# Causal attention: how the 1/sum of the softmax gets into the turned exponentials

## Chip, cores and metric

The kernel runs on one core of a Trainium2 chip. The metric is the device time of one execution in microseconds; the median of several runs is compared. The kernel is one program of many stages, of which the attention stage is one.

## What is computed

A first block (two recurrent mixers and a mixture of experts) is followed by a second one, which projects its input and feeds an attention, a state-space mixer and a gated linear recurrence. The change lies in the attention of the second block, cut here to what matters (1024 positions, 8 heads of 64, all float32):

```python
def fox_attention(q, k, v, log_f, q_g, k_g):
    q = rms_norm(q, q_g)
    k = rms_norm(k, k_g)
    c = jnp.cumsum(log_f.astype(jnp.float32), axis=1)
    ...
    def one_block(args):           # 128 queries of every head
        q_i, c_i, blk = args
        logits = jnp.einsum('bhqd,bhkd->bhqk', q_i, kt) * scale + (c_i[..., :, None] - ck[:, :, None, :])
        logits = jnp.where(kpos[None, :] <= qpos[:, None], logits, -jnp.inf)
        p = jax.nn.softmax(logits.astype(jnp.float32), axis=-1)
        return jnp.einsum('bhqk,bhkd->bhqd', p, vt)
    ...
y_att = fox_attention(q, k, v, log_f, q_norm_g, k_norm_g) * jax.nn.silu(z_att)
```

## The kernel before

`attention` (L2759) is a stage of its own. Queries and keys come already normed and scaled from DRAM, 66 rows a head: 64 of the head and two that carry the cumulated gates, so that one product gives the logits. The work is cut into 64 **units** `(h, t)` (L2769): head h and the tile t of 128 queries, with t+1 blocks of 128 keys. The order is written out: for each pair of heads, for `few` = 0 to 3, for both heads, a small tile `t = few` and a large one `t = 7 - few`. So the units come in 16 periods of four (small, large, small, large), and a period has few+1 and 8-few blocks twice.

What is done to a unit n, and by which engine:

- **score(n)**, PE: one or two products of up to 512 columns (L2851), and a bfloat16 product that adds -1e30 above the diagonal (L2853). Small units (even n) go to the PSUM tile `small`, large ones to one of two halves of `large`. It waits until the exponentials of an earlier unit have left that place.
- **reduce**, DVE (L2934): the negated maximum of the rows into `stat`.
- **exp**, ACT (L2907): exponentials of the scores to `p` in SBUF (four buffers), with the row sum as a second result, which is read out by a second instruction. It waits for the maximum and for the buffer (`turned`, L2906).
- **share**, DVE: the reciprocal of the sum (L2939), a drain, and then `share`, the identity times that reciprocal, a diagonal of 128x128 (L2943, four buffers).
- **turn(n)**, PE (L2856 to L2865): for each block of 128 keys a product with the block of `p` as the stationary operand and the diagonal as the moving one. The result is the block turned and divided by the row's sum. Blocks go in groups of up to four to one of two PSUM banks `pt`; a group waits until ACT has copied the group two before it.
- **copy**, ACT (L2899): each group from `pt` to `pT` in SBUF (six units deep).
- **weigh(n)**, PE (L2867 to L2877): only for every second head, both heads of the pair at once: V times `pT` into the one PSUM tile `po`. It waits for the copies, and for the gate of the weigh before it (`o_made`, L2871), as `po` has one buffer.
- **gate**, DVE (L2926): `po` times the gate to `res`, which SP stores when 8 tiles are done.

Each engine has one queue in the order of a loop. In step n the orders are: PE: score(n+3), turn(n), weigh(n-1). ACT: copies of n, exp(n+3). DVE: reduce(n+3), share(n+2), gate(n-2). Weighs come for the third and fourth unit of each period. So in the first step of a period, PE scores a large unit, turns a small one, and then weighs the large last unit of the period before it; that weigh waits for a gate which DVE has behind the reduce of the large unit just scored and behind a share.

```python
for n in range(-3, N + 1):      # PE, L2879
    if n + 3 < N: score(n + 3)
    if 0 <= n < N: turn(n)
    if n - 1 in weighed: weigh(n - 1)
```

Before the first unit PE turns the values of each head pair by transposes of 128x128 blocks, with the block as stationary and the identity as moving operand (L2838). Transposes in this form are used in other stages too, by the routed experts among them (L2523). Scalings of SBUF tiles by columns on DVE are found at L877 (one column) and L2951 (two columns). The next stage's first loads are issued on SP from within this stage (`next_loads`, L2825).

Of the kernel before, what the change touches and what calls it, by code (L numbers as in the profile page):

```python
# [11 lines left out]
ALU = mybir.AluOpType  # L12
ACT = mybir.ActivationFunctionType
AX = mybir.AxisListType
P = 128
# [54 lines left out]
def chunks(n, size=BANK):  # L70

    return [(a, min(size, n - a)) for a in range(0, n, size)]
# [2686 lines left out]
def attention(nc, consts, proj, at, mix, next_loads):  # L2759
# [9 lines left out]
    units = [(2 * i + hh, t) for i in range(QT) for few in range(NT // 2) for hh in range(2) for t in (few, NT - 1 - few)]  # L2769
    N = len(units)  # L2770
    groups = [chunks(t + 1, GROUP) for _, t in units]
    turns = [sum(len(g) for g in groups[:n]) for n in range(N + 1)]
    weighed = {}
# [3 lines left out]
    with Stage(nc, "attn") as st:  # L2777
# [4 lines left out]
        p = st.sb("p", [P, 4, SEQ])  # L2782
        pT = st.sb("pT", [P, 6, NT, P])
        res = st.sb("res", [P, 2, SEQ])
        share = st.sb("share", [P, 4, P])
        after = st.sb("after", [P, P])
        after_b, ident_b = st.sb("after_b", [P, P], BF16), st.sb("ident_b", [P, P], BF16)
        stat = st.sb("stat", [P, 8, 3])
        large = st.psum("large", [P, 2, 2 * BANK])
        small = st.psum("small", [P, BANK])  # L2790
        pt = st.psum("pt", [P, 2, BANK])
# [2 lines left out]
        v_loaded = [st.sem(f"v_loaded{i}") for i in range(QT)]  # L2794
        z_loaded, mask_made = st.sem("z_loaded"), st.sem("mask_made")
        stored = [st.sem(f"stored{u}") for u in range(2)]
        v_turned, v_made, scored, peak, p_made, share_made, turned, pT_made, o_ready, o_made = (
            st.sem(n) for n in ("v_turned", "v_made", "scored", "peak", "p_made", "share_made", "turned", "pT_made",
                                "o_ready", "o_made"))
        block = st.block()  # L2800

        def scores(n):
            return small[:, :] if n % 2 == 0 else large[:, n // 2 % 2, :]

        @block.sync
        def _(sp):
            def queries_keys(h):
                for j, name in enumerate(("q", "k")):
                    sp.dma_start(qk[:, h % 4, j, :], at[name][h]).then_inc(qk_loaded[h % 4], 16)

            for i in range(QT):
                sp.dma_start(vf[:, i, :], proj[ROW2_V + i * P:ROW2_V + (i + 1) * P, :]).then_inc(v_loaded[i], 16)
                if i == 1:
                    queries_keys(0)
                    queries_keys(1)
            sp.dma_start(zg[:], proj[ROW2_ZA:ROW2_ZA + WID, :].rearrange("(i p) t -> p i t", p=P)).then_inc(z_loaded, 16)
            queries_keys(2)
            queries_keys(3)
            for i in range(QT):
                if i < QT - 2:  # L2820
                    sp.wait_ge(scored, 16 * (i + 1))
                    queries_keys(2 * i + 4)
                    queries_keys(2 * i + 5)
                if i == QT - 2:
                    next_loads(sp)  # L2825
                sp.wait_ge(o_made, NT * (i + 1))
                sp.dma_start(mix[i * P:(i + 1) * P, :], res[:, i % 2, :]).then_inc(stored[i % 2], 16)
            for u in range(2):
                sp.wait_ge(stored[u], 16 * (QT // 2))

        @block.tensor
        def _(pe):
            for i in range(QT):
                pe.wait_ge(v_loaded[i], 16)
                if i >= 2:
                    pe.wait_ge(v_made, i - 1)
                for t in range(NT):
                    op = nc.tensor.transpose(large[:, i % 2, t * P:(t + 1) * P], vf[:, i, t * P:(t + 1) * P], consts["ident"][:, :])  # L2838
                op.then_inc(v_turned, 1)
            pe.wait_ge(mask_made, 1)  # L2840

            def score(n):
                h, t = units[n]
                if n % 2 == 1 and n < 4:
                    pe.wait_ge(v_made, 3 + n // 2)
                elif n >= 2:
                    pe.wait_ge(p_made, n - 1 if n % 2 == 0 else n - 3)
                pe.wait_ge(qk_loaded[h % 4], 32 * (h // 4 + 1))
                b = scores(n)
                for a, size in chunks((t + 1) * P):  # L2850
                    nc.tensor.matmul(b[:, a:a + size], qk[:, h % 4, 0, t * P:(t + 1) * P], qk[:, h % 4, 1, a:a + size],  # L2851
                                     start=True, stop=a + size <= t * P)
                nc.tensor.matmul(b[:, t * P:(t + 1) * P], ident_b[:, :], after_b[:, :], start=False, stop=True)\  # L2853
                    .then_inc(scored, 1)

            def turn(n):  # L2856
                pe.wait_ge(share_made, n + 1)
                for j, (a, size) in enumerate(groups[n]):
                    g = turns[n] + j
                    if g >= 2:  # L2860
                        pe.wait_ge(pT_made, g - 1)
                    for k in range(size):
                        op = nc.tensor.matmul(pt[:, g % 2, k * P:(k + 1) * P], p[:, n % 4, (a + k) * P:(a + k + 1) * P],
                                              share[:, n % 4, :], start=True, stop=True)
                    op.then_inc(turned, 1)  # L2865

            def weigh(n):  # L2867
                (h, t), k = units[n], weighed[n]
                pe.wait_ge(pT_made, turns[n + 1])
                if k >= 1:  # L2870
                    pe.wait_ge(o_made, k)  # L2871
                for j in range(t + 1):
                    for hh in range(2):
                        rows = slice(hh * HEAD, (hh + 1) * HEAD)
                        op = nc.tensor.matmul(po[rows, 0:P], v[:, h // 2, j, rows],
                                              pT[:, (n - 2 + 2 * hh) % 6, j, :], start=(j == 0), stop=(j == t))
                op.then_inc(o_ready, 1)  # L2877

            for n in range(-3, N + 1):  # L2879
                if n + 3 < N:  # L2880
                    score(n + 3)
                if 0 <= n < N:
                    turn(n)
                if n - 1 in weighed:
                    weigh(n - 1)
# [24 lines left out]
        @block.vector  # L2910
        def _(dve):
            nc.vector.tensor_tensor(after[:, :], consts["upto"][:, :], consts["ident"][:, :], ALU.subtract)
            nc.vector.tensor_copy(ident_b[:, :], consts["ident"][:, :])
            dve.drain()
            nc.vector.tensor_scalar(after_b[:, :], after[:, :], -1e30, None, ALU.mult).then_inc(mask_made, 1)

            def gate(n):
                (h, t), k = units[n], weighed[n]
                i = h // 2
                dve.wait_ge(o_ready, k + 1)  # L2920
                if k == 0:
                    dve.wait_ge(z_loaded, 16)
                if i >= 2 and k % NT == 0:
                    dve.wait_ge(stored[i % 2], 16 * (i // 2))
                at = slice(t * P, (t + 1) * P)
                nc.vector.tensor_tensor(res[:, i % 2, at], po[:, 0:P], zg[:, i, at], ALU.mult)\  # L2926
                    .then_inc(o_made, 1)

            for n in range(-3, N + 2):
                m = n + 3  # L2930
                if m < N:
                    dve.wait_ge(scored, m + 1)
                    size = (units[m][1] + 1) * P
                    nc.vector.tensor_reduce(stat[:, m % 8, 0:1], scores(m)[:, 0:size], AX.X, ALU.max, negate=True)\  # L2934
                        .then_inc(peak, 1)
                m = n + 2
                if 0 <= m < N:
                    dve.wait_ge(p_made, m + 1)
                    nc.vector.reciprocal(stat[:, m % 8, 2:3], stat[:, m % 8, 1:2])  # L2939
                    dve.drain()  # L2940
                    if m >= 4:
                        dve.wait_ge(turned, turns[m - 3])
                    nc.vector.tensor_scalar(share[:, m % 4, :], consts["ident"][:, :], stat[:, m % 8, 2:3], None, ALU.mult)\  # L2943
                        .then_inc(share_made, 1)
                if n - 2 in weighed:
                    gate(n - 2)

# [871 lines left out]
```

## Time and profile before

| what | value |
|---|---|
| median of 3 runs | 4291.36 us (4289.26 to 4294.37) |
| span of the profiled execution | 4293.8 us; no other time is given for it |
| PE busy | 3714.3 us, 87% |
| PE weight loads busy | 2991.0 us, 70% |
| DVE busy | 2647.7 us, 62% |
| ACT busy | 2043.4 us, 48% |
| POOL busy | 884.2 us, 21% |
| attention stage, within the span | about 3733 to 3947 us |

The engines are PE (TensorE; PEld is its weight loads), DVE (VectorE), ACT (ScalarE), POOL (GpSimd) and SP (SyncE, which issues transfers). Busy time is that in which an instruction of the engine runs. Matmuls overlap each other, so the spacing of their starts says more than the duration of one. The profile's views used here are: windows (a stretch and its length; the busy us, with the number of instructions, of PE, PEld, DVE, ACT and POOL in it; the clock that TensorE was granted as a part of 2.4 GHz; DMA share and GB/s), groups by line (busy time, mean duration, idle time of the engine just before them and what ended it), waits, and the timeline (instructions in order of time; consecutive ones of a line are merged, with their count as xN and the time from the start of the first to the end of the last). In groups of PE, `a<-b,c` names b as the moving and c as the stationary operand. A float32 product of two general operands has two records in the trace for each matmul of the program; a transpose has one.

### The profile page before, as it was taken

What the parts mean: (1) busy time and instruction counts of PE and PEld (TensorE: products, weight loads), DVE (VectorE), ACT (ScalarE), POOL (GpSimd) and SP (SyncE); (2) the same over time, 40 slices, a digit from 0 to 9 for tenths busy, and PEclk for the clock granted to TensorE, in tenths of its full rate; (3) what the DMA queues carried; (4) which work ended last, traced back from release to release, by engine and by line L of the source; (5) the groups of instructions that cost most, each with busy time, mean ns of one, the idle gap of its engine ahead of it and who ended that gap; (6) DMA issues with size and microseconds to landing.
All of it is one profiled execution on the core that took longest, in us unless ns stands there. A gap on an engine that the chain in (4) does not pass through costs nothing. (4 is left out here: it accounts for less than half of the span.)

```text
span 4293.8 us, 94368 instructions
## 1 busy us (share of the span) xinstructions
PE 3714.3 (87%) x35780; PEld 2991.0 (70%) x35781; DVE 2647.7 (62%) x4120; ACT 2043.4 (48%) x2839; POOL 884.2 (21%) x801
## 2 busy tenths in 40 slices
PE   4998899578785878899999999999859999888779
PEld 0898788577675756477777767777647777666667
DVE  2588688455554656377777767777676674033731
ACT  1577566222221242277777767777641222144720
POOL 3000000233433004233223223222222333100000
PEclk6999899899997889899999999999979999999989
DMA  8255354421211553698999999555453222312452
GB/s 300 72 173 171 97 175 133 136 63 53 80 43 61 168 186 77 224 318 252 310 340 342 341 341 323 118 111 111 100 161 91 79 74 93 114 53 68 129 167 79
DMA packets 523528, 679.21 MB, mean 158 GB/s; under 512 B 77200, under 2 KB 423952, under 8 KB 520144
## 3 DMA queue, kind: packets, MB, share of 16 engines
q1 hardware_dynamic: 483360, 532.85, 38.5%
q0 software_dynamic: 39376, 140.20, 13.3%
q8 instruction: 242, 3.96, 0.4%
q10 hardware_dynamic: 480, 1.62, 0.1%
q14 instruction: 70, 0.57, 0.0%
HBM read 500.38 MB, written 174.19 MB: 157 GB/s over the span
## 5 line engine op out<-in xcount | busy, mean ns | idle before, releaser
L2646 DVE TENSOR_TENSOR routed_w_low<-moe_exp_w,routed_w_high 128x1024 fp32r<-128x1024 f32 x516 | 607.0, 1217 | 54.5 <-ACT routed_w_high L2582 54.2
L2582 ACT CAST routed_w_high<-moe_exp_w 128x1024 fp32r x516 | 514.8, 1045 | 91.8 <-DMA moe_exp_w<-in_exp_w_up_dram 56.2
L2556 PE MATMUL routed_p_gu<-routed_w_high,routed_x_high 128*128 128x512 f32 x1024 | 419.4, 410 | 0.0
L2556 PE MATMUL routed_p_gu<-routed_w_low,routed_x_high 128*128 128x512 f32 x1024 | 408.2, 399 | 0.0
L2556 PE MATMUL routed_p_gu<-routed_w_high,routed_x_low 128*128 128x512 f32 x1024 | 407.9, 398 | 0.0
L2500 POOL DMA_INDIRECT total<-routed_y,routed_yidx x128 | 211.5, 1652 | 843.3 <-ACT routed_y L2607 401.0
L548 PE MATMUL front_ps<-front_a_high,front_w_high 128*128 128x320 f32 (+1 forms) x1120 | 362.7, 324 | 16.4 <-DVE front_w_low L785 13.3
L548 PE MATMUL front_ps<-front_a_high,front_w_low 128*128 128x320 f32 (+1 forms) x1120 | 354.2, 316 | 0.0
L548 PE MATMUL front_ps<-front_a_low,front_w_high 128*128 128x320 f32 (+1 forms) x1120 | 354.1, 316 | 0.0
L3487 PE MATMUL pre_ps<-pre_a_high,pre_w_high 128*128 128x512 f32 x720 | 287.3, 399 | 12.3 <-ACT pre_xb L3614 6.6
L3487 PE MATMUL pre_ps<-pre_a_low,pre_w_high 128*128 128x512 f32 x720 | 281.5, 391 | 0.0
L3487 PE MATMUL pre_ps<-pre_a_high,pre_w_low 128*128 128x512 f32 x720 | 281.3, 391 | 0.0
L2539 PE MATMUL routed_p_y<-routed_wd,routed_hT_rest 128*128 x512 | 262.6, 594 | 0.0
L548 PEld LDWEIGHTS front_ps<-front_a_high,front_w_high 128*128 128x128 f32 x1120 | 213.6, 191 | 35.3 <-DVE front_w_low L785 17.9
L1427 POOL TENSOR_TENSOR rwmix_TT<-rwmix_at,rw_mask 64x256 f32<-64x256 f32 (+1 forms) x60 | 43.5, 724 | 934.0 <-DVE rwmix_at L1328 928.2
L2556 PEld LDWEIGHTS routed_p_gu<-routed_w_high,routed_x_low 128*128 128x128 f32 x1024 | 194.1, 190 | 47.3
L2556 PEld LDWEIGHTS routed_p_gu<-routed_w_low,routed_x_high 128*128 128x128 f32 x1024 | 195.1, 191 | 41.5
L2556 PEld LDWEIGHTS routed_p_gu<-routed_w_high,routed_x_high 128*128 128x128 f32 x1024 | 195.0, 190 | 41.7
L548 PEld LDWEIGHTS front_ps<-front_a_low,front_w_high 128*128 128x128 f32 x1120 | 213.4, 191 | 1.3
L548 PEld LDWEIGHTS front_ps<-front_a_high,front_w_low 128*128 128x128 f32 x1120 | 213.2, 190 | 0.0
L2491 POOL DMA_INDIRECT moe_xg<-yn,moe_idx x129 | 164.5, 1276 | 113.9 <-DVE moe_idx L2635 64.8
L3487 PEld LDWEIGHTS pre_ps<-pre_a_high,pre_w_high 128*128 128x128 f32 x720 | 135.8, 189 | 45.4 <-issue 15.1
(541 smaller groups left out, 8421.5 us busy)
## 6 DMA issues: line engine op xcount, KB each, us to landing
moe_exp_w<-in_exp_w_gate_dram SPq DMA_DIRECT2D x64, 1024.0 KB
moe_exp_w<-in_exp_w_up_dram SPq DMA_DIRECT2D x64, 1024.0 KB
routed_wd<-in_exp_w_down_dram SPq DMA_DIRECT2D x64, 1024.0 KB
front_wt<-in_w_in_dram SPq DMA_DIRECT2D x70, 512.0 KB, 4.4
mod_w<-in_w_mod_dram SPq DMA_DIRECT2D x24, 1024.0 KB, 18.2
pre_wt<-in_w_in_dram SPq DMA_DIRECT2D x44, 512.0 KB, 4.1
out_a<-mix SPq DMA_DIRECT2D x24, 512.0 KB, 4.1
proj<-pre_xv SPq DMA_DIRECT2D x16, 512.0 KB, 2.6
```

The costliest lines, as they stand in the source:

```text
L548: op = nc.tensor.matmul(ps[:, s % 2, c, 0:size], w_part[:, s % 2, k, :], a_part[:, k, first + c * size:first + (c + 1) * size], start=(k = ...
L1427: nc.gpsimd.tensor_tensor(combos(TT[u][:])[to, es], combos(at[u][:])[at_rows, es], mask(MASK_LEVEL, at_rows, es), ALU.mult)
L2491: nc.gpsimd.indirect_dma_start(xg[:, b % 2, :], None, yn, bass.IndirectOffsetOnAxis(ap=idx[b][:, :], axis=0))\
L2500: nc.gpsimd.indirect_dma_start(total, bass.IndirectOffsetOnAxis(ap=yidx[b % 2][:, :], axis=0), y[:, b % 2, :], None, compute_op=ALU.add).t ...
L2539: op = nc.tensor.matmul(p_y[:, h, :], hT_rest[:, :], wd[:, bass.ds(e % WS, 1), 1, cols], start=False, stop=True)
L2556: op = nc.tensor.matmul(p_gu[:, :], x_part, w_part[:, k, :], start=(k == 0 and i == 0), stop=(k == KD - 1 and i == 2))
L2582: nc.scalar.copy(w_high[:, q * KQ:(q + 1) * KQ, :].rearrange("p k m -> p (k m)"), wgu[:, bass.ds(e % WS, 1), q * KQ:(q + 1) * KQ].rearrang ...
L2646: nc.vector.tensor_tensor(w_low[:, at, :].rearrange("p k m -> p (k m)"), wgu[:, bass.ds(e % WS, 1), at].rearrange("p o k j m -> p (o k j m)"),
L3487: op = nc.tensor.matmul(ps[:, u, a:a + n], w_part[:, u, k, :], a_part[:, k, a:a + n], start=(k == 0 and j == 0), stop=(k == KD - 1 and j = ...
```

## The change

The diagonal `share` goes. DVE scales the whole row of exponentials in `p` by the reciprocal in place, (t+1) x 128 columns in one instruction, and PE turns the blocks by transposes against the identity. The semaphore is renamed, and DVE no longer waits for `turned` before it writes.

```diff
--- before.py
+++ after.py
@@ -2782,7 +2782,6 @@
         p = st.sb("p", [P, 4, SEQ])
         pT = st.sb("pT", [P, 6, NT, P])
         res = st.sb("res", [P, 2, SEQ])
-        share = st.sb("share", [P, 4, P])
         after = st.sb("after", [P, P])
         after_b, ident_b = st.sb("after_b", [P, P], BF16), st.sb("ident_b", [P, P], BF16)
         stat = st.sb("stat", [P, 8, 3])
@@ -2794,8 +2793,8 @@
         v_loaded = [st.sem(f"v_loaded{i}") for i in range(QT)]
         z_loaded, mask_made = st.sem("z_loaded"), st.sem("mask_made")
         stored = [st.sem(f"stored{u}") for u in range(2)]
-        v_turned, v_made, scored, peak, p_made, share_made, turned, pT_made, o_ready, o_made = (
-            st.sem(n) for n in ("v_turned", "v_made", "scored", "peak", "p_made", "share_made", "turned", "pT_made",
+        v_turned, v_made, scored, peak, p_made, shared, turned, pT_made, o_ready, o_made = (
+            st.sem(n) for n in ("v_turned", "v_made", "scored", "peak", "p_made", "shared", "turned", "pT_made",
                                 "o_ready", "o_made"))
         block = st.block()
 
@@ -2854,14 +2853,14 @@
                     .then_inc(scored, 1)
 
             def turn(n):
-                pe.wait_ge(share_made, n + 1)
+                pe.wait_ge(shared, n + 1)
                 for j, (a, size) in enumerate(groups[n]):
                     g = turns[n] + j
                     if g >= 2:
                         pe.wait_ge(pT_made, g - 1)
                     for k in range(size):
-                        op = nc.tensor.matmul(pt[:, g % 2, k * P:(k + 1) * P], p[:, n % 4, (a + k) * P:(a + k + 1) * P],
-                                              share[:, n % 4, :], start=True, stop=True)
+                        op = nc.tensor.transpose(pt[:, g % 2, k * P:(k + 1) * P], p[:, n % 4, (a + k) * P:(a + k + 1) * P],
+                                                 consts["ident"][:, :])
                     op.then_inc(turned, 1)
 
             def weigh(n):
@@ -2938,10 +2937,9 @@
                     dve.wait_ge(p_made, m + 1)
                     nc.vector.reciprocal(stat[:, m % 8, 2:3], stat[:, m % 8, 1:2])
                     dve.drain()
-                    if m >= 4:
-                        dve.wait_ge(turned, turns[m - 3])
-                    nc.vector.tensor_scalar(share[:, m % 4, :], consts["ident"][:, :], stat[:, m % 8, 2:3], None, ALU.mult)\
-                        .then_inc(share_made, 1)
+                    size = (units[m][1] + 1) * P
+                    nc.vector.tensor_scalar(p[:, m % 4, 0:size], p[:, m % 4, 0:size], stat[:, m % 8, 2:3], None, ALU.mult)\
+                        .then_inc(shared, 1)
                 if n - 2 in weighed:
                     gate(n - 2)
 
```

## Rows read from the trace of the kernel before

**Rows 1.** The page's first line: the span.

```profile
span 4293.8 us, 94368 instructions
```

**Rows 2.** Windows: the attention stage.

```profile
3747.00:3947.00 200.00, 180.73 (x1390) 137.49 (x1388) 77.56 (x222) 94.01 (x226) 0.00 (x0) 0.97 0.20 53
```

**Rows 3.** Groups by line, the turning (busy us, mean ns, idle before).

```profile
L2863 PE MATMUL attn_pt<-attn_share,attn_p 128*128 128x128 f32 x576 | 79.4, 284 | 0.6 <-ACT attn_pT L2899 0.6
```

**Rows 4.** Waits in the attention stage: us in total, times, longest.

```profile
PE attn_po L2875 <- DVE attn_res L2926: 15.1, 11, 1.8
```

**Rows 5.** Timeline of one chain, few = 0: start us, us, instruction, idle before.

```profile
3847.38 0.22 PE L2853 MATMUL attn_large<-attn_after_b,attn_ident_b 128*128 128x128 bf16 x1
...
3847.64 1.22 DVE L2934 TENSOR_REDUCE attn_stat<-attn_large 128x1 f32<-128x1024 f32 x1 [2.14 <-PE attn_large L2853]
...
3848.78 0.15 DVE L2939 RECIPROCAL attn_stat<-attn_stat 128x1 f32<-128x1 f32 x1
3848.90 1.11 ACT L2907 ACTIVATE attn_p<-attn_large,attn_stat 128x1024 f32<-128x1024 f32 x1 [0.66 <-DVE attn_stat L2934]
3849.01 0.29 DVE L2943 TENSOR_SCALAR attn_share<-ident,attn_stat 128x128 f32<-128x128 f32 x1
3849.22 0.28 DVE L2926 TENSOR_TENSOR attn_res<-attn_po,attn_zg 128x128 f32<-128x128 f32 x1
...
3849.65 2.40 PE L2875 MATMUL attn_po<-attn_pT,attn_v 128*64 128x128 f32 x20 [1.76 <-DVE attn_res L2926]
3849.91 0.19 ACT L2907 ACTIVATION_READ_ACCUMULATOR attn_p<-attn_large,attn_stat 128x1 f32 x1
```

**Rows 6.** Timeline of PE: the large weighs of few = 1, 2 and 3.

```profile
3763.27 1.97 PE L2875 MATMUL attn_po<-attn_pT,attn_v 128*64 128x128 f32 x32 [1.41 <-DVE attn_res L2926]
3775.84 1.75 PE L2875 MATMUL attn_po<-attn_pT,attn_v 128*64 128x128 f32 x28 [1.05 <-DVE attn_res L2926]
3788.05 1.53 PE L2875 MATMUL attn_po<-attn_pT,attn_v 128*64 128x128 f32 x24 [0.70 <-ACT attn_pT L2899]
```

**Rows 7.** Timeline of PE: eight products, and what follows them.

```profile
3753.06 2.00 PE L2863 MATMUL attn_pt<-attn_share,attn_p 128*128 128x128 f32 x16
3754.90 0.59 PE L2851 MATMUL attn_large<-attn_qk 66*128 66x512 f32 x1
```

**Rows 8.** Timeline of PE, expert stage: eight transposes, and what follows them.

```profile
2006.35 1.04 PE L2523 MATMUL routed_p_x<-ident,moe_xg 128*128 128x128 f32 x8
2007.15 0.48 PE L2556 MATMUL routed_p_gu<-routed_w_high,routed_x_high 128*128 128x512 f32 x1
```

**Rows 9.** Scalings of SBUF by columns: a group by line; one line (ns min/median/max).

```profile
L877 DVE TENSOR_SCALAR front_rb<-front_rb,front_cols 128x640 f32<-128x640 f32 x8 | 4.4, 553 | 0.8
L2951 DVE TENSOR_SCALAR pre_yb<-pre_xb,pre_xtaps,pre_xbias x12: 811/2734/2885, 3376.5 to 3602.7; 128x1024 f32<-128x1024 f32 x12
```

**Rows 10.** Timeline of the change from few = 2 to 3, PE and ACT.

```profile
3778.54 1.55 PE L2863 MATMUL attn_pt<-attn_share,attn_p 128*128 128x128 f32 x12
...
3779.74 0.86 ACT L2899 COPY attn_pT<-attn_pt 128x512 f32<-128x512 f32 x2 [3.49 <-PE attn_pt L2863]
...
3780.48 0.70 ACT L2907 ACTIVATE attn_p<-attn_small,attn_stat 128x512 f32<-128x512 f32 x1
...
3781.79 1.02 PE L2851 MATMUL attn_small<-attn_qk 66*128 66x512 f32 x2
```

**Rows 11.** Windows (columns as rows 2), the two falls of the clock.

```profile
3849.00:3857.00 8.00, 7.35 (x41) 6.43 (x42) 1.47 (x6) 2.13 (x4) 0.00 (x0) 0.57 0.25 83
3914.00:3918.00 4.00, 4.00 (x34) 3.52 (x35) 0.00 (x0) 0.29 (x2) 0.00 (x0) 0.57 0.00 0
```

**Rows 12.** Timeline and windows (columns as rows 2): the V transposes.

```profile
3743.77 3.44 PE L2838 MATMUL attn_large<-ident,attn_vf 128*128 128x128 f32 x16 [5.75 <-DMA attn_vf<-proj]
...
3745.00:3746.00 1.00, 1.00 (x7) 1.00 (x6) 0.00 (x0) 0.23 (x1) 0.00 (x0) 0.50 1.03 414
...
3747.00:3748.00 1.00, 1.00 (x7) 0.75 (x6) 0.29 (x1) 0.76 (x1) 0.00 (x0) 1.00 0.66 270
```

## Prediction

> **What bounds the kernel now.** The profiled execution has a span of 4293.8 us [rows 1]. No separate time is given for it; the three runs shown have a median of 4291.36, 2.4 lower, so I take differences in the span and subtract them from the median. 0.2% of it, about what a measurement of this kernel can tell from no change, is 8.6 us.
>
> The change is in the attention stage alone, so I read that stage first by windows: from 3747 to 3947 us TensorE is busy 181 of 200 us, DVE 78, ACT 94, POOL not at all, and TensorE's granted clock averages 0.97 of 2.4 GHz [rows 2]. TensorE sets the pace. The groups by line show where: L2863, the turning by products, is the costliest with 79.4 us, in 576 records [rows 3]. The stage turns 8 heads x 36 blocks = 288 blocks of 128x128, so each product is two records. L2943, the diagonal, is one instruction of 0.29 us a unit on DVE [rows 5], 19 us in all.
>
> Then the waits: TensorE stands idle for DVE 15.1 us, in front of L2875, the product with V [rows 4]. The timeline gives the pattern [rows 5]. The 64 units go in 16 periods of four: a small tile of few+1 blocks and a large one of 8-few, for two heads, few = 0 to 3. Once in a period PE scores a large unit (its mask product at T0 = 3847.38), turns a small one, and must then wait with the large weigh until DVE has done reduce, reciprocal, share and gate: 3849.65 - 3847.38 = 2.27 us after T0. The reduce is shorter for the larger few. The idle that the chain leaves is 1.76, 1.41, 1.05 and 0.70 us for few = 0, 1, 2, 3 [rows 5, 6]; the last is put down to ACT, but the gate ends at the same moment. So one turn of each period (few+1 blocks, 40 blocks in all 16) already lies beside a DVE chain. The other 248 blocks lie on TensorE's path.
>
> **The change, part by part.**
>
> Products become transposes. At full clock eight products start at 3753.06 and the next matmul at 3754.90: 0.230 us a block [rows 7]. Eight transposes of the same shape with the same identity, in the expert stage, take 2006.35 to 2007.15: 0.100 us a block; by (1.04 - 0.27)/7 of the same row it is 0.110 [rows 8]. The next matmul may start a little early, so I take a saving of 0.120 a block (ends 0.113 and 0.130). 248 x 0.120 = **29.8 us** (28.0 to 32.2). The 40 hidden blocks give nothing: 40 x 0.12 = 4.8 us of TensorE work become idle time.
>
> The Trainium skill (TensorE: Matmul & The Clock Gate, Part 4: PE-mode transpose) gives about 275 ns for one transpose in a kernel. As a pace that would exceed the 0.230 of a product, and this term would be an estimated 248 x 0.045 = 11 us lost; rows 8 agree with the figure as a duration (0.27) but not as a spacing (this is rival 3).
>
> The diagonal goes, the row scaling comes. A tensor_scalar with one column scalar takes 0.29 us at 128 columns [rows 5] and 0.553 at 640 [rows 9], so 0.52 ns a column and some 0.75 us at 1024. With two scalars 1024 columns take 0.811, my upper end while POOL is idle. Mean size is 576 columns: 0.52 us x 64 = 33 us for 19, 14 us more on an engine that is busy 78 of 200. What matters is its place:
> - In the DVE chain above the scaling is that of a small unit (few+1 blocks): longer by few x 0.067 us, 0.4 us over four periods, **1.6 us** in all. This is on the path.
> - Large scalings come once exp of that unit is done, in front of the next reduce. For the 1024 size and T the mask product of that unit: reduce 0.26 after T, exp 1.26 later for 1.11, the sum's read-out 0.19, reciprocal 0.23, scaling 0.7: T + 3.7 [rows 5, 9]. PE in that time issues the mask product (0.06) and turns a block (0.12), scores a small unit (0.27), turns 8 blocks (0.9), weighs a small unit (4 of the records that go 32 in 1.97 us, 0.2 [rows 6]) and scores 1024 columns (four records; two take 1.02 and one 0.59, so 0.43 each, 1.7 [rows 7, 10]): the next large mask product is at T + 3.3, its reduce 0.26 later at 3.6. So DVE just keeps up; I cost this at nothing, its cover being that PE work. If the cover is gone it is 0.1 to 0.3 us in four to eight periods, 2 us.
> - The DVE wait for the turned diagonal goes, with nothing behind it; ACT's own wait on the same count stays and guards p.
>
> ACT does not get faster. Where it gets late: with few = 2 the small score of the next period (L2851, at 3781.79) waits for an exp that follows the copies. Turning starts at 3778.54, copies at 3779.74, exp at 3780.48 for 0.70 plus 0.2 for the sum's read-out [rows 5]: ready 2.8 us after the start, needed 3.25 after [rows 10]. Afterwards copies start some 0.5 earlier (ready 2.3), but nine blocks fewer costs bring PE there 1.08 earlier (2.17): a wait of 0.1. With few = 3 the second group of a large turn waits about 0.2 for the copy of the small turn before it. Four head pairs: **1.2 us** (0 to 13; the upper end is 0.4 us at each of the 32 small scores).
>
> The clock. It fell to half twice in the stage, right behind such idle gaps: one of 1.76 us at 3849, one of the 1.41 kind at 3914; the stretches had 0.57 on average [rows 11]. About 10 us at half cost 5. After the change the gaps are 1.88, 1.72, 1.54 and 1.38 us: (before) + 0.12 x blocks turned + 0.067 x few. Two in the eight gaps of 1.4 or more fell; now all 16 are about that size, so I expect four falls, two more, at 2.5 us each, a little less since part lies beside the chain: **4 us** (-5, if no gap falls, to +15).
>
> Sum: 29.8 - 1.6 - 1.2 - 4 = 23.0 us. 4293.8 - 23.0 = 4270.8 in the span, **4268** against the median. Loads, stores and the later stages are the same; SP's next loads wait for gates and come earlier with them.
>
> **Rivals.**
>
> 1. ACT becomes the pace (17%). PE turns six blocks in 0.7 us and ACT copies them in 0.86 [rows 10]. For: the slack above shrinks from 0.45 us to none. Against: only two groups come at a time, with two buffers and a score of 1 to 1.8 us behind them. At the upper end of 13 us the gain is 11: 4280.
>
> 2. The clock stays down, the slower side (4%). Place: the 16 gaps. If each fall lasts two of the lengths seen (6.8 us at half, 3.4 lost), k falls cost 3.4k - 5, against a gain of 26.2 before the clock. It decides from k = 10 on; from 12 the kernel is slower by 0.2%, at 16 it is 49 lost, 4314. For: gaps in every period, more of them with little work on both sides. Against: the V transposes. From 3743.77 to 3747.04 PE did nothing but 16 transposes, and the clock went from 0.50 to 1.00 meanwhile [rows 12], so transposes do count as work.
> The same Part 4 of the Trainium skill's page TensorE: Matmul & The Clock Gate says that transposes do not bring on the full clock, which would make this rival the likely one; rows 12 speak against it here.
>
> 3. The transposes are not cheaper (2%, the change not doing what it says): paced at their duration of 0.273 us, 248 x 0.043 = 10.7 us lost, with the other terms 4305. Rows 8 speak against it.
>
> 4. The scaling is slow (2%): L2951 takes 2.73 us for 1024 columns where POOL works beside it [rows 9]. 0.9 us more on the small and 0.6 to 1.3 on the large scalings in 16 periods is 24 to 35: 4287 to 4300. POOL is idle here [rows 2].
>
> 5. Better (4%): no fall of the clock and the 0.130 spacing: 32.2 - 1.6 - 0 + 5 = 36: 4256.
>
> My forecast has the remaining 71%, 4261 to 4277. The range of 4258 to 4282 takes in rival 1 and part of 5 and leaves out some 15%. Faster by over 0.2%: forecast, 1 and 5, less a tail, 0.91; within: 4 and that tail, 0.04; slower: 2 and 3, 0.05.
>
> **What would show it.** The turning line with 288 records instead of 576 and a spacing of 0.10 to 0.12 us; the span between large weighs down from some 12.3 to 10.6 us; PE idle before L2875 up from 18 to some 24 us; L2943's successor at 285 ns (128 columns) to 0.75 us (1024), 33 us in all, with reduces starting 0.26 after the mask product as before. PE idle before L2851 on ACT above 3 us would be rival 1, a granted clock under 0.9 over the stage rival 2. A stage shorter by over 30 us, or by under 14, would make my sum wrong.

## The result, and the profile after

The changed kernel takes 4271.1 us (median of 4 runs, 4266.07 to 4274.89), the kernel before 4292.15 us (4 runs). The ratio is 0.995 with an interval of 0.9937 to 0.9963: 21 us faster, 16 to 27 by the interval, more than the 0.2% set as the bound. Forecast were 4268 and a range of 4258 to 4282.

The two profiled executions differ by more, 4293.8 to 4267.6 us. Not all of that is the change: the first score of the attention stage begins at 3746.9 in the one and at 3740.3 in the other, behind stages with the same code. Over the twelve executions profiled for this study that moment lies at 3746.9 to 3756.3 in the four whose kernel turns by products, and at 3731.8 to 3743.4 in the eight with transposes. The two groups do not overlap, and no run here shows why. I do not count it to the change, as the medians differ by about what the stages do, within 5 us: 21.1 to 17.7 here, and 58.8 to 55.7, 18.4 to 18.3 and 29.7 to 29.4 in three of the runs below. So what follows is measured on the stage itself, from the first score to the last product with V. These are the windows of that stretch, first of the kernel before, then of the changed one (stretch, length, busy us of PE, PEld, DVE, ACT and POOL, granted clock, DMA share, GB/s):

```profile
3746.90:3949.00 202.10, 182.29 (x1411) 138.69 (x1409) 77.87 (x224) 94.01 (x226) 0.00 (x0) 0.97 0.20 52
```

```profile
3740.30:3924.70 184.40, 156.93 (x1123) 107.03 (x1121) 92.39 (x224) 93.52 (x226) 0.00 (x0) 0.92 0.21 57
```

The stage is 17.7 us shorter. TensorE has 25 us less busy time, DVE 14.5 more, ACT the same, and the mean clock fell from 0.97 to 0.92. The fall of the clock is the surprise of the case. Groups by line in the changed kernel (busy us, mean ns, idle before), to be held against [rows 3] and [rows 4]:

```profile
L2862 PE MATMUL attn_pt<-ident,attn_p 128*128 128x128 f32 x288 | 45.5, 286 | 1.3 <-ACT attn_pT L2898 1.3
L2874 PE MATMUL attn_po<-attn_pT,attn_v 128*64 128x128 f32 x576 | 44.3, 305 | 25.0 <-DVE attn_res L2925 25.0
...
L2941 DVE TENSOR_SCALAR attn_p<-attn_p,attn_stat 128x128 f32<-128x128 f32 (+3 forms) x64 | 33.3, 520 | 5.3 <-issue 0.4
```

288 records in place of 576; the turning went from 79.4 to 45.5 us busy. The scaling takes 33.3 us. TensorE now waits 25.0 us before the product with V, against 18.4 over the same stretch of the kernel before (15.6 put down to DVE, 2.8 to ACT at the same moment, see [rows 6]). [Rows 4] leaves out the last such wait, of 0.5 us. So 15 of the 16 waits in the changed kernel are gaps of 1.4 us or more, and the last is 0.5 us as before.

The spacing, in the timeline of PE in the changed kernel, where eight transposes are followed by a product with V (as [rows 7] for the products):

```profile
3890.43 1.04 PE L2862 MATMUL attn_pt<-ident,attn_p 128*128 128x128 f32 x8
3891.40 0.44 PE L2874 MATMUL attn_po<-attn_pT,attn_v 128*64 128x128 f32 x4
```

0.97 us for eight, 0.121 us a block, where the product had 0.230: 0.109 saved. And the DVE chain of a period with few = 0, as [rows 5]:

```profile
3881.66 0.22 PE L2852 MATMUL attn_large<-attn_after_b,attn_ident_b 128*128 128x128 bf16 x1
...
3881.91 1.22 DVE L2933 TENSOR_REDUCE attn_stat<-attn_large 128x1 f32<-128x1024 f32 x1 [1.01 <-PE attn_large L2852]
...
3883.06 0.15 DVE L2938 RECIPROCAL attn_stat<-attn_stat 128x1 f32<-128x1 f32 x1
...
3883.29 0.29 DVE L2941 TENSOR_SCALAR attn_p<-attn_p,attn_stat 128x128 f32<-128x128 f32 x1
3883.49 0.28 DVE L2925 TENSOR_TENSOR attn_res<-attn_po,attn_zg 128x128 f32<-128x128 f32 x1
...
3883.92 0.55 PE L2874 MATMUL attn_po<-attn_pT,attn_v 128*64 128x128 f32 x6 [1.93 <-DVE attn_res L2925]
```

From mask product to weigh it is 2.26 us, as before; only the gap in it has grown, as the one block is turned sooner. The gaps of the next periods, in the timeline of PE (few counts the period whose small unit has just been turned, here 1, 2, 3 and 0; the same count underlies [rows 6]):

```profile
3805.69 3.52 PE L2874 MATMUL attn_po<-attn_pT,attn_v 128*64 128x128 f32 x32 [1.75 <-DVE attn_res L2925]
3818.09 1.75 PE L2874 MATMUL attn_po<-attn_pT,attn_v 128*64 128x128 f32 x28 [1.57 <-DVE attn_res L2925]
3828.91 1.53 PE L2874 MATMUL attn_po<-attn_pT,attn_v 128*64 128x128 f32 x24 [1.40 <-DVE attn_res L2925]
3839.78 2.20 PE L2874 MATMUL attn_po<-attn_pT,attn_v 128*64 128x128 f32 x20 [1.92 <-DVE attn_res L2925]
```

Forecast were 1.72, 1.54, 1.38 and 1.88. The first of these weighs takes 3.52 us where [rows 6] has 1.97 for the same 32 records: it ran at half clock. Windows around the weigh at 3792.51, behind another gap of 1.93:

```profile
3792.00:3793.00 1.00, 0.49 (x6) 0.52 (x8) 0.36 (x2) 0.96 (x2) 0.00 (x0) 0.62 0.00 0
3793.00:3794.00 1.00, 1.00 (x12) 1.00 (x11) 0.00 (x0) 0.00 (x0) 0.00 (x0) 0.50 0.00 0
...
3799.00:3800.00 1.00, 1.00 (x5) 0.41 (x4) 0.00 (x0) 0.00 (x0) 0.00 (x0) 0.96 0.85 344
```

Windows of 2 us over the whole stage show five such falls in the changed kernel, where the kernel before has two. Four of the five begin in a window in which a gap ended (3792, 3805, 3839, 3883); the fifth is at 3751, among the first units, behind a wait of 0.56 us for exponentials that ended at 3750.45.

To compare stages whose clocks differ, I multiply the length by the mean clock and call it the length **free of the clock**: 202.1 x 0.97 = 196.0 and 184.4 x 0.92 = 169.6 us. It takes all of the stage as going with the clock, which a wait for DVE does not, and 0.01 of the clock is 2 us, so differences of 1 or 2 us in this measure say little.

### The profile page after: what moved, and what is told of

Its sections match the earlier page's. It is cut to its first block and busy times, and to the rows that moved or that the text cites. A ratio compares the mean times of both kernels' runs of the same rounds, so it can differ in the third digit from the quotient of the medians.

```text
span 4267.6 us, 93792 instructions
## 1 busy us (share of the span) xinstructions
PE 3691.2 (86%) x35492; PEld 2958.7 (69%) x35493; DVE 2666.3 (62%) x4120; ACT 2045.7 (48%) x2839; POOL 901.5 (21%) x801
## 5 line engine op out<-in xcount | busy, mean ns | idle before, releaser
L2646 DVE TENSOR_TENSOR routed_w_low<-moe_exp_w,routed_w_high 128x1024 fp32r<-128x1024 f32 x516 | 607.5, 1218 | 33.1 <-ACT routed_w_high L2582 30.6
L2582 ACT CAST routed_w_high<-moe_exp_w 128x1024 fp32r x516 | 515.1, 1045 | 68.8 <-DMA moe_exp_w<-in_exp_w_up_dram 29.7
L2500 POOL DMA_INDIRECT total<-routed_y,routed_yidx x128 | 230.2, 1798 | 836.6 <-ACT routed_y L2607 346.9
```

The lines of the kernel that those rows point to most:

```text
L2500: nc.gpsimd.indirect_dma_start(total, bass.IndirectOffsetOnAxis(ap=yidx[b % 2][:, :], axis=0), y[:, b % 2, :], None, compute_op=ALU.add).t ...
L2582: nc.scalar.copy(w_high[:, q * KQ:(q + 1) * KQ, :].rearrange("p k m -> p (k m)"), wgu[:, bass.ds(e % WS, 1), q * KQ:(q + 1) * KQ].rearrang ...
L2646: nc.vector.tensor_tensor(w_low[:, at, :].rearrange("p k m -> p (k m)"), wgu[:, bass.ds(e % WS, 1), at].rearrange("p o k j m -> p (o k j m)"),
```

## The experiments

Theory: TensorE's spacing of the blocks gives the gain; one DVE chain a period hides a turn and costs what the small scaling adds; the gaps that this chain leaves bring down the clock, which takes back part. Rivals: the diagonal and its wait gave the gain; ACT is the next pace; the work on DVE as such costs time; the falls of the clock come from the transposes or from chance. The edits are shown cut and are, where nothing else is said, made in the changed kernel. Every stage is read from one profiled execution.

**The transposes alone.**

```diff
-nc.vector.tensor_scalar(p[:, m % 4, 0:size], p[:, m % 4, 0:size], stat[:, m % 8, 2:3], None, ALU.mult)
+nc.vector.tensor_scalar(share[:, m % 4, :], consts["ident"][:, :], stat[:, m % 8, 2:3], None, ALU.mult)
```

> The change's transposes alone: DVE writes the diagonal as before, nothing reads it, and the exponentials are turned unscaled, so the division by the row sums is left out of the result. If the time comes from TensorE's pace and the scaling costs only what it adds to the one DVE chain a period (my sum), this run is 1 to 2 us below the changed kernel, about 4269, with 0.121 us a block and idle time of TensorE before the product with V of about 24 us. If the large scalings also delay the reduces behind them, it is 5 us or more below the changed kernel, 4266 or less.

4276.35 us beside 4299.73 for the kernel before on that chip: ratio 0.9945 (0.9925 to 0.9965), 23 us. The stage:

```profile
3743.40:3920.00 176.60, 150.56 (x1123) 102.99 (x1121) 77.98 (x224) 93.57 (x226) 0.00 (x0) 0.96 0.24 60
```

Free of the clock it is 169.5 us, the changed kernel 169.6. The idle time before the product with V is 23.5 us, 1.5 below the changed kernel: that is the small scaling in the chain (forecast 1.6), and the rest of the 33 us of scaling costs nothing that this can tell. In the profiles themselves the stage is 7.8 us shorter; that is the clock, 0.96 for 0.92, with four falls.

**The scaling alone.**

```diff
-op = nc.tensor.transpose(pt[...], p[...], consts["ident"][:, :])
+op = nc.tensor.matmul(pt[...], p[...], consts["ident"][:, :], start=True, stop=True)
```

> The scaling in place alone: the blocks are still turned by matrix products, against the plain identity. By my sum the products keep 0.230 us a block, the scaling adds 1.6 us on the DVE chain, and the time is 4292 to 4295, no faster than before. If part of the gain came from the diagonal and its wait going away, it is 4287 or less. If a product with the identity of the same constant tile is itself cheaper than with the diagonal, the spacing shows it.

4304.4 beside 4299.73 us: ratio 1.0007 (0.9995 to 1.0019). The forecast of 4292 to 4295 was for a chip on which the kernel before takes 4292; here it takes 7.6 us more. The stage:

```profile
3756.30:3958.50 202.20, 181.02 (x1411) 137.36 (x1409) 92.61 (x223) 94.11 (x226) 0.00 (x0) 0.98 0.20 52
```

That is 198.2 us free of the clock, and the idle time before the product with V is 20.0 us, 1.6 above the kernel before, as forecast for the small scaling. Eight products with the plain identity still go from 3812.46 to 3814.29:

```profile
3812.46 2.00 PE L2862 MATMUL attn_pt<-ident,attn_p 128*128 128x128 f32 x16
3814.29 1.67 PE L2850 MATMUL attn_large<-attn_qk 66*128 66x512 f32 x4
```

0.229 us a block. So neither the diagonal nor its wait gave anything; all of the gain is in the transposes.

**The gate at the head of DVE's step**, in the changed kernel and in the kernel before:

```diff
 for n in range(-3, N + 2):
+    if n - 2 in weighed:
+        gate(n - 2)
     m = n + 3
     ...
-    if n - 2 in weighed:
-        gate(n - 2)
```

> The changed kernel with DVE's gate moved from the end of its step to the head, in front of the reduce. The weigh that it releases then waits for nothing: the 25 us of idle time of TensorE before the product with V should go to under 3, and with the gaps the five falls of the clock should go to one or two. My theory: 25 us of idle and some 7 us of clock, less up to 6 us of waits that come next (small scores and copies on ACT), so 4242 to 4250. If the falls of the clock don't come from the gaps, they stay four or more and the time is 4250 to 4255. If ACT is already the pace behind the gaps, TensorE waits for ACT instead and the time is 4260 or more.

> The kernel before with the same move of the gate and nothing else. The 18 us of idle time before the product with V should go, and the two falls of the clock with it (up to 5 us): 4269 to 4275. The 40 blocks that were turned beside the DVE chain now lie on TensorE's path in both kernels, so against the run with the changed kernel the difference should be 288 x 0.109 = 31 us less the new waits, 25 to 31 us, larger than the 21 between the kernels as they are. If ACT is the next pace, the difference is under 20.

4240.9 and 4281.35 beside 4299.73 us: ratios 0.9861 (0.9839 to 0.9882) and 0.9956 (0.994 to 0.9972). The stages, one window each:

```profile
3736.60:3883.00 146.40, 143.22 (x1123) 97.32 (x1121) 94.12 (x224) 93.44 (x226) 0.00 (x0) 1.00 0.27 72
```

```profile
3748.90:3932.70 183.80, 182.69 (x1410) 137.72 (x1409) 80.11 (x223) 94.33 (x226) 0.00 (x0) 0.96 0.21 57
```

With the change the stage drops from 184.4 to 146.4 us. 23.2 of the 38 us are idle time (169.6 to 146.4 free of the clock), 14.8 the clock: it is 1.00 over the whole stage, with all 288 transposes in it, and windows of 2 us show no fall. The wait is gone from the changed kernel:

```profile
PE attn_po L2874 <- DVE attn_res L2925: 0.5, 1, 0.5
```

In the kernel before, the stage began at half clock, which was low since before it; behind that nothing fell. Free of the clock it is 176.4 us, and the difference between the two is 30.0: 288 x 0.109 = 31.4 less a wait or two. So the 40 hidden blocks came out of cover. With the clock in it the difference is 37.4 us between the stages and 40.5 between the medians, where I had 25 to 31; the clock that began low in the kernel before takes about 7 of it, and the rest is not settled. Of the changed kernel with the moved gate the profiled execution, 4226.43 us, is the fastest of five. ACT is not the pace even here, with 93 us busy of 146: TensorE waits 1.3 us for copies and 1.3 for exponentials. The gain was larger than forecast: 58.8 us between the medians and 55.7 between the stages, where the lower end of my range was 50 below the kernel before. I had put up to 6 us on new waits, where all waits for ACT together are 2.6, and 7 on the clock, where 15 lay. In the kernel before the move gave 18.4 us between the medians, as forecast (17 to 23).

**The gap filled.**

```diff
 pe.wait_ge(pT_made, turns[n + 1])
+if k % 2 == 1:
+    for _ in range(16):
+        nc.tensor.matmul(pt[:, (turns[n + 1] + 1) % 2, 0:P], ident_b[:, :], after_b[:, :], start=True, stop=True)
```

> The changed kernel with 16 bfloat16 matmuls of 128 columns put into each of the 16 gaps, in front of the wait for the gate; their result is overwritten unread. They take about 1 us of a gap of 1.4 to 1.9, so the DVE chain still sets the end of the gap and nothing is saved but the clock. If the falls of the clock come from the gaps, there are none or one in the stage instead of five, and the stage (first score to last product with V) goes from 184.4 to about 170 us. If they come from something else (the transposes, the stretches of scores with 66 rows), four or more stay and the stage stays at 180 or more. If the fill delays the weighs, the gaps' ends move and the stage is longer with the clock up.

```profile
3742.70:3915.40 172.70, 160.14 (x1379) 113.24 (x1377) 92.35 (x223) 93.53 (x226) 0.00 (x0) 0.99 0.21 61
```

```profile
3789.72 0.28 PE L2862 MATMUL attn_pt<-ident,attn_p 128*128 128x128 f32 x1
3789.83 1.06 PE L2871 MATMUL attn_pt<-attn_after_b,attn_ident_b 128*128 128x128 bf16 x16
3791.83 0.88 PE L2877 MATMUL attn_po<-attn_pT,attn_v 128*64 128x128 f32 x12 [0.94 <-DVE attn_res L2928]
```

The first fence is the window of its stage, the second the timeline of one filled gap. 256 useless matmuls make the stage 11.7 us shorter than in the changed kernel: same chain, and the gaps end within 0.1 us of where they did behind the mask product (2.17 for 2.26 us at few = 0), but the clock is 0.99 and falls once instead of five times, at 3753, behind a wait for exponentials that was not filled. I had expected about 170 us. The median is 4259.03 beside 4288.68 us, ratio 0.993 (0.9906 to 0.9954). This is the run that shows the clock's part by itself. Free of the clock it is 171.0, near the 169.6 of the changed kernel.

**The gate behind the reduce, but ahead of the scaling.**

```diff
     nc.vector.tensor_reduce(...)
+    if n - 2 in weighed:
+        gate(n - 2)
     ...
     nc.vector.tensor_scalar(p[...], ...)
-    if n - 2 in weighed:
-        gate(n - 2)
```

> The changed kernel with the gate moved only in front of the reciprocal and the scaling, still behind the reduce. The DVE chain of each period loses reciprocal and small scaling: 0.43 us at few = 0 to 0.63 at few = 3, 8.5 us over 16 periods, with the gaps at about 1.5, 1.3, 1.05 and 0.8. Taken free of the clock the stage goes from 169.6 to 161 us; with gaps like those of the kernel before it should have two falls or fewer. If the gap were set by something else than the chain on DVE, it stays.

```profile
3740.60:3909.30 168.70, 149.07 (x1123) 101.54 (x1120) 92.44 (x223) 93.52 (x226) 0.00 (x0) 0.97 0.24 62
```

The gaps are 1.49, 1.25, 1.00 and 0.76 us, 16.9 in all (13.9 put down to DVE, 3.0 to ACT), 8.1 less than 25.0 as forecast. There are three falls, where I had two or fewer. Free of the clock the stage is 163.6; I had 161. The median is 4259.2 beside 4288.68, ratio 0.9931 (0.9908 to 0.9953). The chain does set the gap, and the reduce is the larger part of it.

**Scalings doubled**, of the large units in one kernel, of the small ones in the other:

```diff
 nc.vector.tensor_scalar(p[:, m % 4, 0:size], p[:, m % 4, 0:size], stat[:, m % 8, 2:3], None, ALU.mult)
+if m % 2 == 1:      # == 0 in the other kernel
+    dve.drain()
+    nc.vector.tensor_scalar(p[:, m % 4, 0:size], p[:, m % 4, 0:size], 1.0, None, ALU.mult)
```

TensorE is released (`shared`) behind the second of the two.

> The changed kernel with every large unit scaled twice, the second time by 1.0: 32 more scalings of 0.55 to 0.75 us, with a drain. The trace of the changed kernel shows DVE idle for 0.43 us (896 columns) and 1.0 to 1.4 us (the other sizes) before the reduce that heads the chain, so these scalings are covered: free of the clock the stage grows by 2 us (0 to 4), not by the 22 us of added DVE work. If the large scalings were on the path, it would grow by 10 or more.

> The changed kernel with every small unit scaled twice, the second time by 1.0: 32 more scalings of 0.29 to 0.49 us, with a drain. Half of them lie in the DVE chain of a period: 16 x 0.47 = 7.5 us longer free of the clock, all of it as idle time before the product with V (25 to about 32 us), though this adds less DVE work (13 to 15 us) than the run with the large ones twice. If total DVE work counted and not its place, this run would lose less than that one.

```profile
3740.20:3928.80 188.60, 159.84 (x1122) 108.44 (x1121) 110.25 (x256) 93.31 (x226) 0.00 (x0) 0.92 0.21 56
```

```profile
3731.80:3936.00 204.20, 171.55 (x1122) 116.80 (x1120) 102.47 (x256) 93.38 (x226) 0.00 (x0) 0.85 0.18 51
```

The windows are of the stages, first with the large, then with the small units scaled twice. One profiled execution each: 4274.81 and 4289.1 us, beside a median of 4288.68 for the kernel before.

The large ones add 18 us of DVE work and 3.9 to the stage free of the clock (173.5; the upper end of my expectation of 0 to 4, and 2 us of it can be rounding), with the idle time at the product with V hardly changed, 25.7 us. Their cover can be seen in DVE's timeline of the changed kernel, where the reduces at the head of the chain wait for PE behind the scalings of 896 and of 1024 columns:

```profile
3880.15 0.75 DVE L2941 TENSOR_SCALAR attn_p<-attn_p,attn_stat 128x1024 f32<-128x1024 f32 x1
3881.91 1.22 DVE L2933 TENSOR_REDUCE attn_stat<-attn_large 128x1 f32<-128x1024 f32 x1 [1.01 <-PE attn_large L2852]
...
3892.51 0.69 DVE L2941 TENSOR_SCALAR attn_p<-attn_p,attn_stat 128x896 f32<-128x896 f32 x1
3893.63 1.09 DVE L2933 TENSOR_REDUCE attn_stat<-attn_large 128x1 f32<-128x896 f32 x1 [0.43 <-PE attn_large L2852]
```

The small ones add 10 us of DVE work (I had 13 to 15). The gaps become 2.23, 2.12, 2.01 and 1.90 us, 30.9 in all: 5.9 more (I had 7.5; the second scaling follows the first more closely than I took). But the stage is 204.2 us long, 19.8 more than in the changed kernel and 2 more than in the kernel before. Free of the clock it is 173.6; the other 30.6 us are the clock, which averages 0.85 and falls ten times. That is 4.0 more than the changed kernel where I had 7.5, and no more than with the large ones doubled: this measure halves a wait that falls into a stretch at half clock, and does not tell the two places apart. The idle time does, with 5.9 us more for 10 us of work against 0.7 for 18, and so does the length, with 19.8 us more against 4.2. The place of the work decides, and the clock triples what it costs.

**Both kernels once more**, unaltered:

> The changed kernel once more, unaltered, to see how far the count of falls of the clock in the stage is the kernel's and how far chance. If the gaps bring them, there are again four to seven falls, behind gaps of 1.4 us or more, and the stage takes 180 to 190 us. If the five were chance, as few as two can come, with a stage near 174 us.

> The kernel before once more, unaltered. With gaps of 0.7 to 1.76 us I expect one to three falls and a stage of 199 to 204 us. If the falls were chance in both kernels, the count here would reach that of the changed kernel.

```profile
3736.00:3916.40 180.40, 153.42 (x1122) 104.81 (x1121) 92.59 (x223) 93.47 (x226) 0.00 (x0) 0.94 0.21 58
```

```profile
3753.70:3954.60 200.90, 181.44 (x1411) 138.06 (x1409) 77.85 (x223) 94.12 (x226) 0.00 (x0) 0.98 0.19 53
```

The changed kernel falls five times again, the kernel before twice (a window at the very start is the end of an earlier stretch). The stages differ by 20.5 us, 27.3 free of the clock (169.6 to 196.9). The whole executions took 4262.98 and 4300.81 us, one each.

All stages side by side, the idle time being that of TensorE before the product with V:

| kernel | idle, us | falls | clock | stage, us | free of the clock |
|---|---|---|---|---|---|
| gate at the head, changed | 0.5 | 0 | 1.00 | 146.4 | 146.4 |
| gate at the head, before | 0.5 | 0 (began low) | 0.96 | 183.8 | 176.4 |
| gap filled | 9.9 | 1 | 0.99 | 172.7 | 171.0 |
| gate behind the reduce | 16.9 | 3 | 0.97 | 168.7 | 163.6 |
| before | 18.4 | 2 | 0.97 | 202.1 | 196.0 |
| before, again | 18.4 | 2 | 0.98 | 200.9 | 196.9 |
| scaling alone | 20.0 | 1 | 0.98 | 202.2 | 198.2 |
| transposes alone | 23.5 | 4 | 0.96 | 176.6 | 169.5 |
| changed | 25.0 | 5 | 0.92 | 184.4 | 169.6 |
| changed, again | 25.2 | 5 | 0.94 | 180.4 | 169.6 |
| large scaled twice | 25.7 | 5 | 0.92 | 188.6 | 173.5 |
| small scaled twice | 30.9 | 10 | 0.85 | 204.2 | 173.6 |

## Why the prediction was right, and which term was off

Right: the sign, the range, and the likeliest case. 23.0 us were forecast; 21.1 were measured between the medians, 17.7 and 20.5 between the stages of two pairs of profiles. Term by term:

- **Products to transposes, 29.8 us.** The mechanism is shown by the two halves of the change run alone. The saving is 0.109 us a block, not 0.120, so 248 x 0.109 = 27.0. I had taken 0.100 for a transpose from the start of the next matmul; the 0.110 of the same row was nearer, and here it is 0.121. That 248 blocks count and 40 do not is borne out: the 40 came out of cover when the gate was moved (30.0 us between those two stages).
- **The small scaling in the chain, 1.6 us.** 1.5 by the idle time with and without it among the transposes, 1.6 among the products.
- **The large scalings, nothing.** Right, and with more cover than I worked out: 0.43 to 1.4 us idle on DVE before the chain's reduce, where I had it just keeping up. My T + 3.3 for the next large mask product was too early: at few = 0 it comes 4.5 us behind T (3877.16 to 3881.66 in the changed kernel), with 16 records of a weigh in between and not 4. The scaling ends at T + 3.7, as worked out.
- **New waits on ACT, 1.2 us.** TensorE waits 2.4 us for copies and exponentials, 1.4 before: 1.0 more. The size is right by luck, as the place is wrong: I had put 0.3 us into each of the four head pairs, at few = 2 and 3. The five waits that there are (three for copies, 1.3 us, and two for exponentials, 1.1 us) lie in the first 11 and the last 10 us of the stage; from 3760 to 3915 TensorE waits for ACT not once, so those four waits did not come. Rival 1 did not happen, and did not even in the stage of 146 us.
- **The clock, 4 us.** This is the term that was mis-sized. The loss is length less length free of the clock: 14.8 and 10.8 us in the two profiles of the changed kernel, 6.1 and 4.0 in the two of the kernel before. That is 8.7 and 6.8 us more, against 4. The gaps were forecast to 0.05 us; I expected four falls and there were five, and one lasted from 3751 to 3762. The count that it was forecast from was slightly off too: before the change seven gaps, not eight, are of 1.4 us or more, and after it 15 and not 16.
- **Rival 2, the slower side.** I had it decide from ten falls on, and put the kernel slower by 0.2% from twelve. With the small scalings doubled there are ten, and the stage is already 2 us longer than before the change. The rival was nearer than its 4%: 0.3 to 0.5 us more in each gap would have eaten the whole gain. The mechanism was the gaps and not the transposes, as [rows 12] had it.
- **Rival 4, the slow scaling.** It did not happen: the scalings take 33.3 us, the 33 forecast. Its times were added up without the 4 us of the clock; with them 24 to 35 us more give 4292 to 4303, not 4287 to 4300.

Before the clock I had forecast 27.0 us; free of the clock the stages give 26.4 and 27.3. The smaller saving a block should have made it 24.5; the 2 us between are within the rounding of that measure, and I leave them open.

Which gaps bring a fall is not chance alone. In the two profiles of the changed kernel a fall comes at all six gaps of few = 0 (1.9 us), at two of the eight of few = 1 (1.55 to 1.75), and at none of the sixteen of few = 2 and 3 (1.4 to 1.6); the remaining two falls lie among the first units, behind waits of 0.56 and 0.76 us. The length does not decide by itself: with the small scalings doubled, three gaps of 1.90 us at few = 3 bring none, while the four of 2.01 at few = 2 bring four. Why is not settled. Nor are the two kernels' counts ordered by idle time everywhere: the scaling alone has one fall in 20.0 us, and the kernel before two in 18.4.

## What to carry to other kernels

Once TensorE is sped up, look at the waits that its work used to cover: the 40 blocks turned beside a DVE chain gave nothing until the chain was cut, and a one-buffered result whose reader stands behind unrelated work on its engine is cut by moving the reader to the head of the step. Cost such a gap at its length and at what the lower clock behind it takes. In the changed kernel 25 us of idle time came with another 11 to 15 us of clock, with 30.9 us it was 30.6. The version with the change and the gate at the head beats both kernels: 4240.9 beside 4299.73 us, ratio 0.9861.

## What the hardware did that I had not expected

- The clock's loss grows much faster than the idle time: with 0.5 us of idle in the stage of the changed kernel it is nothing, with 17 to 20 us it is 4 to 6, with 23.5 us 7, with 25 us 11 to 15, with 30.9 us 30.6. 256 matmuls without use, about 1 us in each gap, make the stage 11.7 us shorter.
- Transposes do not hold the clock down. The stage with 288 of them and no gaps runs at 1.00, among products of other kinds, and in [rows 12] the clock rose to 1.00 while TensorE did nothing but V transposes. The Trainium skill (TensorE: Matmul & The Clock Gate, Part 4: PE-mode transpose) says that the full clock does not engage for them; these two measurements decide against it here.
- The matrix product with the plain identity costs the same as with the diagonal, 0.229 us a block against 0.230, and has two records as well; the transpose form takes 0.121.
